# Rounds of scores between the projection slots of a gated recurrence, and a weight ring that runs on over the experts

## The reference

```python
def hgrn2_mixer(h, w_in, w_out, o_norm, lower_bound):
    q, f_logit, i_in, g = jnp.split((h @ w_in).astype(f32), 4, axis=-1)   # 4 x 1024 columns
    log_f = jnp.log(lb + (1.0 - lb) * jax.nn.sigmoid(f_logit))
    k = (1.0 - lb) * jax.nn.sigmoid(-f_logit)
    o = hgrn2_chunkwise(heads(q), heads(k), heads(i_in), heads(log_f))    # 8 heads of 128
    o = rms_norm(o, o_norm) * jax.nn.silu(heads(g))
    return o.reshape(B, S, ...).astype(h.dtype) @ w_out
...
        # b = running sum of log_f; scores[t,s] = sum_d q[t,d] k[s,d] exp(b[t,d] - b[s,d]), s <= t
        scores = jnp.einsum('bhtd,bhsd,bhtsd->bhts', qi, ki, jnp.exp(rel))
...
def moe_ffn(x, router, w_gu, w_down):
    for e in range(N_EXPERTS):                                            # 8 experts, 2 for each token
        y = y + combine[:, e:e + 1] * swiglu(xt, w_gu[e], w_down[e])
```

## Time and profile before

| | us |
|---|---|
| median of 3 runs | 2792.12 (2791.61 to 2793.78) |
| the profiled execution | 2794.28 |
| its span, first to last instruction | 2792.5 |
| TensorE busy | 2479.7 (89%) |
| VectorE busy | 1873.3 (67%) |
| ScalarE busy | 1322.0 (47%) |
| mean granted clock of TensorE | 0.943 |

### The profile page before, as it was taken

The page is one execution under the profiler, slowest core; times in us unless marked ns, Lnnn a source line. Parts: engine busy times, 40 slices in busy tenths (PEclk is TensorE's granted clock), DMA queues, the critical chain, the costliest instruction groups (busy, mean ns, idle before and its releaser), DMA issues.

```text
span 2792.5 us, 44521 instructions
## 1 busy us (share of the span) xinstructions
PE 2479.7 (89%) x17928; PEld 2334.3 (84%) x17928; DVE 1873.3 (67%) x2349; ACT 1322.0 (47%) x1408; POOL 308.8 (11%) x70
## 2 busy tenths in 40 slices
PE   6689789996678799789989788999999999999997
PEld 6579789996578699779978467989898999999996
DVE  5656575648556575742254657888888788888887
ACT  4434333334334233323322334766667676666674
POOL 0000063400000063345500000000000000000000
PEclk9899899998889899989999788999999999999999
DMA  5124135542034145445532014989888889889895
GB/s 204 61 91 150 69 144 182 189 140 103 0 119 146 61 167 182 151 144 179 186 120 77 1 61 157 361 327 343 320 331 337 335 325 335 335 325 342 327 341 206
DMA packets 77071, 556.56 MB, mean 199 GB/s; under 512 B 8544, under 2 KB 8672, under 8 KB 9952
## 3 DMA queue, kind: packets, MB, share of 16 engines
q1 hardware_dynamic: 75888, 547.45, 53.2%
q10 hardware_dynamic: 1008, 6.49, 0.6%
HBM read 552.86 MB, written 1.05 MB: 198 GB/s over the span
## 4 chain that ended last, share of the span: by engine, by line
PE 59%; DVE 5%; issue 2%; ACT 2%; DMA 0%; DVEq 0%; ACTq 0%
PE ps L1104 11%; PE ps L1106 11%; PE ps L1105 11%; PE ps L665 6%; PE ps L666 6%; PE ps L667 6%; PE ps L746 2%; PE ps L719 1%; PE ps L1144 1%; PE ps L1098 1%; DVE wlo L1229 1%; PE ps L800 1%; ACT whi L437 1%; PE ps L760 1%; PE ps L797 1%
## 5 line engine op out<-in xcount | busy, mean ns | idle before, releaser
L437 ACT ACTIVATE whi<-raw 128x2048 fp32r<-128x2048 f32 x519 | 992.0, 1914 | 737.8 <-PE ps L667 559.2
L1229 DVE TENSOR_TENSOR wlo<-raw,whi 128x2048 fp32r<-128x2048 f32 x453 | 1035.1, 2290 | 252.9 <-ACT whi L437 250.8
L665 PE MATMUL ps<-hh,whi 128*128 128x256 f32 x2336 | 679.7, 291 | 111.3 <-DVE hl L1297 94.8
L666 PE MATMUL ps<-hl,whi 128*128 128x256 f32 x2336 | 673.6, 288 | 0.0
L667 PE MATMUL ps<-hh,wlo 128*128 128x256 f32 x2336 | 672.9, 288 | 0.0
L665 PEld LDWEIGHTS ps<-hh,whi 128*128 128x128 f32 x2336 | 460.5, 197 | 117.8 <-issue 107.7
L1104 PE MATMUL ps<-whi,hh 128*128 128x256 f32 x1792 | 523.9, 292 | 15.3 <-issue 11.7
L1106 PE MATMUL ps<-wlo,hh 128*128 128x256 f32 x1792 | 507.7, 283 | 0.0
L1105 PE MATMUL ps<-whi,hl 128*128 128x256 f32 x1792 | 507.5, 283 | 0.0
L666 PEld LDWEIGHTS ps<-hl,whi 128*128 128x128 f32 x2336 | 460.9, 197 | 0.3
L667 PEld LDWEIGHTS ps<-hh,wlo 128*128 128x128 f32 x2336 | 460.4, 197 | 0.0
(11 more groups left out here) (313 smaller groups left out, 2737.0 us busy)
## 6 DMA issues: line engine op xcount, KB each, us to landing
raw<-stream SPq DMA_DIRECT2D x519, 1024.0 KB, 4.8
work<-w_in ACTq DMA_DIRECT2D x1, 2240.0 KB, 8.4
stage<-stage_consts ACTq DMA_DIRECT2D x4, 512.0 KB, 4.6
work<-mem_in ACTq DMA_DIRECT2D x2, 1024.0 KB, 5.5
x<-x_in SPq DMA_DIRECT2D x1, 1024.0 KB, 4.9
out<-x SPq DMA_DIRECT2D x4, 256.0 KB, 2.3
const<-consts SPq DMA_DIRECT2D x1, 548.5 KB, 5.8
par<-params SPq DMA_DIRECT2D x1, 405.5 KB, 6.4
```

The source lines that it names most:

```text
L437: nc.scalar.activation(whi[hi_at(g)][:, :], raw[g % RAWS][:, :], ACT.Copy).then_inc(hi_ready, 1)
L665: mm(out_ap, hi_w, hi_x, start=start, stop=False, **kw)
L666: mm(out_ap, hi_w, lo_x, start=False, stop=False, **kw)
L1229: V.tensor_tensor(wlo[g % RAWS][:, :], raw[g % RAWS][:, :], whi[hi_at(g)][:, :].bitcast(F32), ALU.subtract).then_inc(lo_ready[g % RAWS], 1)
```

## The change

**Recurrence.** The stream's order of `hg_in` changes: SyncE's loads are written out up to slot 180, and slots 0 to 3 fetch the weights of f, 4 to 7 those of q. The fills stand ahead of the phase. Sigmoids come in iteration 3, the logarithm (one operation a head, with factor and bias on ScalarE) and an Exp of it in iteration 4, keys in 4 (8 operations), the scan in 5. The nine rounds are made in the order `HG_ROUNDS`: diagonal, level 7, 0, 1 to 6. Round k's difference is made in iteration k+5 (rounds 2 and 3 in 6 and 7), its Exp in the same on ScalarE, its products in k+6, its matmuls after slot k+7, its masked copies in k+8. Differences are made with the right sign in two half-width operations (no Abs); level 7 needs no difference, since exp(b[t] - b[t-1]) is the forget factor itself. There are three difference buffers (`hg_d0`, `hg_d1` over the experts' activation buffers, and `hf`), one group of four banks, 4 to 7, for all rounds, and bank 3 for the values, which are turned in four parts after slots 9 to 12 and copied by ScalarE. Slots 8 to 15 are drained by ScalarE. The normalisation behind goes by quarters.

**Experts.** The ring doesn't start over; `few_expert` is written out on all engines (the other branch, which doesn't run, becomes a loop over pairs).

```diff
-        HG_D = [W(16, 8), hf[:, :]]
+        HG_D = [hg_d0[:, :], hg_d1[:, :], hf[:, :]]
+        HG_ROUNDS = ["diag", 7, 0, 1, 2, 3, 4, 5, 6]
...
-        def hi_at(g):
-
-            return (g if g < FIRST + PER_EXPERT else g - PER_EXPERT) % DEPTH
+        def hi_at(g, odd=0):
+
+            return (g + odd * PER_EXPERT) % DEPTH
...
-                    act.wait_ge(slot_used, e * PER_EXPERT + used_before(g))
-                nc.scalar.activation(whi[hi_at(g)][:, :], raw[g % RAWS][:, :], ACT.Copy).then_inc(hi_ready, 1)
+                    act.wait_ge(slot_used, e * PER_EXPERT + (g - DEPTH + 1))
+                nc.scalar.activation(whi[hi_at(g, odd)][:, :], raw[g % RAWS][:, :], ACT.Copy).then_inc(hi_ready, 1)
...
+            def after_hg_slot(s):
+                hg_scores(s - 7)
+                if 9 <= s <= 12:
+                    hg_turn_values(s - 9)
+
+            proj_pe("hg_in", 7, {s: lambda s=s: after_hg_slot(s) for s in range(7, hg.n)})
...
+                if 7 <= s <= 14:
+                    weigh(s - 6)
...
+                if s >= 8:
+                    keep(s - 8)
+                if s in (6, 7):
+                    decays(s - 4)
+                if 9 <= s <= 13:
+                    decays(s - 5)
+                split_lo(hg.g + s + AHEAD)
```

More of the change, by code:

```diff
@@ L365, in at_least, with source_of, expert_pairs @@
                 eng.wait_ge(s, value)
+        def source_of(g):
+            s = g - PHASES["hg_in"].g
+            return g + 4 if 0 <= s < 4 else (g - 4 if 4 <= s < 8 else g)
+        def expert_pairs(eng, body):
+            with eng.Fori(0, EXPERTS // 2) as pair:
+                for odd in range(2):
+                    body(pair * 2 + odd, odd)
         def wait_lo(eng, g, e=0):
@@ L578, in _ @@
+            for c in range(QUARTERS):
+                act.wait_ge(act_step, chain[0] - 3 + c)
+                nc.scalar.activation(W(8 + 2 * c, 2), W(8 + 2 * c, 2), ACT.Exp, scale=-0.5).then_inc(hg_orstd, 1)
             act.dma_start(stage[:, :], stage_consts[STAGE["pool"]]).then_inc(stage_loaded, 16)
@@ L625, in few_expert @@
                         bank, j = (gu.g + s) % BANKS, part * HALF + s
-                        if part == 0 and s == 2 and not first:
+                        if part == 0 and s == 2 and e:
                             few_keep_y(e - 1)
@@ L642, in _, with expert @@
                     nc.scalar.activation(Wc(FEW_GIVE + col, 512 * width), banks(bank, width), ACT.Copy).then_inc(spread_ready, 1)
-                few_expert(0, True)
-                with act.Fori(1, EXPERTS) as e:
-                    few_expert(e, False)
+                for e in range(EXPERTS):
+                    few_expert(e)
                 few_keep_y(EXPERTS - 1)
             with act.Else():
-                with act.Fori(0, EXPERTS) as e:
+                def expert(e, odd):
                     for part in range(2):
@@ L913, in _, with hg_turn_values @@
             norm_pe(4)
[L914 to L915 removed]
+            hg = PHASES["hg_in"]
+            def hg_turn_values(j):
+                pe.wait_ge(banks_drained, hg.e + 9 + j)
+                at_least(pe, hg_kept, j)
                 for tt in range(2):
[L917 to L920 removed]
@@ L923, in _ @@
-            proj_pe("hg_in", 7, {12: hg_turn_values})
-            pe.wait_ge(banks_drained, PHASES["hg_in"].e + PHASES["hg_in"].n)
-            def hg_scores(bank, lhs, rhs, tiles):
-                for h in range(8):
-                    for n, tt in enumerate(tiles):
-                        col = h * len(tiles) + n
-                        last = mm(ps[:, bank + col // 4, (col % 4) * P:(col % 4 + 1) * P], lhs(h, tt[0]), rhs(h, tt[1]), start=True, stop=True)
-                last.then_inc(hg_s, 1)
@@ L1128, in few_down @@
                 g = down.g + s
-                hi, lo = whi[hi_at(g)], wlo[g % RAWS]
+                hi, lo = whi[hi_at(g, e % 2)], wlo[g % RAWS]
                 wait_lo(pe, g, e)
@@ L1155, in few_expert @@
                             few_turn(gu, s - 1, e, part * HALF + s - 1)
-                    if part == 0 and not first:
+                    if part == 0 and e:
                         pe.wait_ge(y_kept, e)
@@ L1161, in few_expert @@
                             few_turn(gu, HALF - 1, e, part * HALF + HALF - 1)
-                        if part == 0 and not first and s in (1, 4):
+                        if part == 0 and e and s in (1, 4):
                             if s == 4:
@@ L1165, in few_expert @@
                             few_spread(e - 1, s // 4, 5)
-                        if part == 1 and s == 1 and not final:
-                            if not first:
+                        if part == 1 and s == 1 and e < EXPERTS - 1:
+                            if e:
                                 pe.wait_ge(y_added, e * 2 + 1)
@@ L1197, in _, with expert @@
                 acc_zero(True, False)
-                with pe.Fori(0, EXPERTS) as e:
+                def expert(e, odd):
                     for part in range(2):
@@ L1701, in _ @@
+            for c in range(QUARTERS):
+                gated(c)
+            sync()
+            staged(normed, to_hi(W(16, 8)), to_lo(W(16, 8)))
             xa(1, "hg_out")
```

353 lines of the change are left out of this document (199 added, 154 removed).

## The result

| | before | after |
|---|---|---|
| median | 2792.61 us (2791.61 to 2793.78, 4 runs) | 2710.49 us (2708.6 to 2710.99, 4 runs) |
| the profiled execution, its span | 2794.28, 2792.5 | 2710.58, 2708.8 |
| mean granted clock of TensorE | 0.943 | 0.948 |

After over before is 0.9705, 95% interval 0.9688 to 0.9721: 82 us less. The forecast was 2706; the time lies 4.5 us above it and inside the range. Between the spans of the two profiled executions the difference is 83.7 us (2792.5 - 2708.8); the sum had said 86.9.

A forecast was written before the change was run, and what follows sets the result against it. TensorE mostly waits for 106 us between the recurrence's projections and some 3 us per expert. Savings of 61.3 + 22.8 + 2.8 = 86.9 us give 2707.4 from the profiled execution, 2705.2 from the median; forecast 2706, range 2698 to 2722.

The forecast's parts named there:

- the sum: Whole kernel: savings in the recurrence, the experts and the last expert's end, 61.3 + 22.8 + 2.8 = 86.9 us.
- The gain in the recurrence: Rounds between projection slots, shorter normalisation: output projection starts at 717.0 instead of 778.33, 61.3 us.
- the first wait: Recurrence: TensorE waits 0.95 us for slot 7's drain, queued on VectorE behind scan, subtraction and remainders.
- The three turns: Recurrence: three turns of the values each wait 1.13 us for ScalarE's previous copy, queued behind Exp.
- no wait of TensorE over 2 us: Sign in the profile after, between slot 0 of the recurrence's input projection and the last round, ending near 699.5.
- the 24 matmuls with the values: Behind the last round: some 5.5 us, priced by the 3.82 us for 16 matmuls.
- The experts: Borders of experts: with the ring running on, 3.3 us less at each of seven borders, 22.8 us.
- late loads: Rival in the experts: weights come late at the borders, 22.8 us given back, 2729; chance 0.05 for experts not getting shorter.
- The end of the last expert: Copy of the last expert's result waits for only one unused slot's rounding and ends at 2763.8: 2.8 us saved.
- The rounds at the lower clock: Rival in the recurrence: rounds cost 5.46 us each and the time is 2716; chance 0.1.
- VectorE as the bound: Rival in slots with rounds: VectorE operations or waits cost 10% more, each slot grows 0.8 to 0.9 us, 2713; chance 0.1.
- Straight code as a loss: Rival in the experts: loading written-out code stalls ScalarE or VectorE, 94 us on top, 2800; chance 0.02.

The follow-up runs named there:

- log_first: The changed kernel with ScalarE's rounding of slot 8's weights moved behind the eight logarithms of iteration 4; 2707.51 us.
- rounds_behind: The changed kernel with its rounds of scores moved behind slot 15 of the projection on all three engines; 2759.47 us.
- dve_extra: The changed kernel with one more VectorE addition, about 1.2 us, in each of iterations 9 to 13 of the recurrence's projection; 2709.79 us.
- unroll_only: The kernel before with the experts written out on ScalarE and VectorE, the ring still starting over with each expert; 2796.93 us.
- after_again: The changed kernel run once more, unedited, as a base for later kernels; 2711.15 us.
- all_three: The changed kernel with value copies ahead of Exp, slot 8's rounding behind the logarithms, and the last expert's four unused slots not taken apart; 2698.58 us.

## Why the prediction was right, point by point

**The gain in the recurrence: right in place and mechanism, 3.5 us too large.** From slot 7's end to the end of the last round the sum had 85.0 us (614.5 to 699.5); the trace has 86.6 (613.22 to 699.85). The step that was off is the first wait, 2.50 and not 0.95. I had followed VectorE from the moment at which slot 0's drain lets it go, and had the scan start when that queue was free; in fact the scan starts at 604.43 with an idle time of 1.99 in front, waiting for the logarithms, which ScalarE takes behind the rounding of slot 8's weights. log_first moved just that and got 1.6 us back. The three turns wait 1.29 each and not 1.13, 0.5 more; TensorE's own work was 0.5 less than its 79.8. By this the prediction's own sign "no wait of TensorE over 2 us" up to the last round failed, at 2.50, without touching the mechanism. Its other signs held (last round's end at 699.85, rounds of 3.8 at 1.00, no Abs, experts of 129.3, no stop at a border), but `hg_out` came 58.9 us earlier and not 61.

From the last round's end to `hg_out` the sum had 17.5; it is 19.6. Nearly all of the difference is the 24 matmuls with the values: 7.2 us and not 5.5. They ran at a granted clock of 0.76. The windows of these matmuls and of the last spread in the changed kernel, and then of the same two in log_first (columns PE busy, granted clock, DMA, GB/s; the third window takes in seven records behind the 48):

```profile
702.40:709.50 7.10, 7.04 (x48) 0.76 0.00 0
...
2680.80:2687.20 6.40, 6.37 (x17) 0.57 0.03 6
```

```profile
701.40:708.40 7.00, 6.92 (x55) 1.00 0.00 0
...
2678.40:2682.20 3.80, 3.72 (x16) 1.00 0.03 6
```

I had priced them by rounds at full clock, and had kept the lower clock for the rounds alone. In the kernel before they took 5.6 us at 1.00, behind the same wait of 2.62, so its trace gave no sign of this term.

**The experts: right.** 22.8 us were forecast; the seven borders gave 23.3 (132.64 - 129.31 at each of six, and 3.4 at the last), 3.33 a border against 3.27, and expert 0, which has no border ahead of it, 0.3. VectorE was in time for the turn: none stands behind a wait. The end of the last expert gave 3.2 and not 2.8. What I had not said is how close the stream now is: I named late loads as an all-or-nothing rival at 2729, and in fact they take nothing in one execution and 2 to 6 us in another (above). By the windows the DMA engines' share rose from 0.89 to 0.91, as estimated.

**The end: missed.** From the last copy to the end nothing is changed, and the sum gave it nothing; the chances spoke of "some us either way through the clock". It took 2.2 us more, because the last spread ran at 0.57 (6.41 us; before 5.18 at 0.71) and the second sum of the final norm took 5.41 us (before 4.52): 1.2 and 0.9. In the executions profiled here the spread takes 3.72 (five kernels), 5.12, 5.18 (before), 5.41 (three), 6.37, 6.41 and 6.46 us, with the same code for it in all of them.

**The rivals.** The rounds at the lower clock didn't come: all nine ran at 1.00, though TensorE stood still for 2.50, 0.94 and three times 1.29 us among them. The Trainium skill's page "TensorE: Matmul & The Clock Gate", section "A second HAM failure mode: psum-queue depth-cycling", tells of a kernel that oscillates between the clocks through brief repeated idle times. Between slots this case's trace doesn't show it; behind the projection rounds_behind does, with idle times of 2.64 and 3.50 around rounds of 5.4 us and a mean clock of 0.73. VectorE as the bound fell with dve_extra. Straight code as a loss fell with unroll_only. The one load of a table on the path took 1.28 us, Exp starting 0.01 us behind it; the switch of 2.66 us, draining included, that the Trainium skill's page "ScalarE: Activation LUTs" gives in "What ACT_TABLE_LOAD costs" doesn't show here. ScalarE after:

```profile
711.63 2.42 ACT L630 ACTIVATE work<-ps,const 128x512 f32<-128x512 f32 x4
714.08 1.28 ACT L633 ACT_TABLE_LOAD   x1
715.37 0.63 ACT L633 ACTIVATE work<-work 128x512 f32<-128x512 f32 x1
```

What held the prediction together is that the terms that failed were small and the two large ones rest on the same kind of working: follow each engine's queue with measured durations, and ask at each step who is last. Some luck is in it too: against 3.5 lost in the recurrence and 2.2 at the end stand 1.3 more in the experts and 1.1 in the untouched start. The 0.8 us that I put on top of the sum (2706 instead of 2705.2) was far too little. The measured median is 5.3 above 2705.2: 3.2 by the sum's error, and 2.1 because the profiled execution before lay 2.2 above the median that I subtracted from, and the one after 0.1 above its own.

## What to carry to other kernels

Work whose steps wait for each other costs least between pieces of work that doesn't wait. Round 7 took 29 us here from its difference (663.96) to the end of its masked copies (693.1), about three times the 10.1 of a round before, and still cost only TensorE's 3.7, because what each engine does for one round fits into the time of a slot and a round. When a ring of buffers is written out for a loop, look at the seam: a ring whose length doesn't divide the loop's reuses a buffer too early once in each pass, and the wait shows up on an engine that has nothing to do with it. And once the order is right, look at what stands ahead of the last waited-for operation in its queue: two moves of a single operation, and leaving out four roundings and remainders that nobody uses, gave another 8 us here.

## What the runs showed that I had not expected

- The length of a wait doesn't decide the clock behind it. In two executions of the same kernel (the changed one and after_again) the last spread follows 3.33 and 3.38 us of idle time and ran at 0.57 (6.41 us) and 0.69 (5.41 us); in log_first it follows 3.30 and ran at 1.00 (3.72 us). The 24 matmuls with the values follow 2.6 us of idle time in all 13 traces. They ran at 1.00 in the three with the old recurrence, in log_first and in rounds_behind, at 0.79 in all_three, and at 0.76 in the other seven (1.6 us). There the two executions of the same kernel agree. What decides the clock was not found; a forecast of this kernel can't be better than these 2 to 4 us.
- Rounds of 128 x 128 float32 matmuls behind idle times of 0.9 to 2.5 us stayed at 1.00 as long as a projection slot stood between them, and fell to 0.73 on average without one. The idle times differ as well: in rounds_behind they are 2.64 us and more, and the one round there behind a shorter one, 1.21, took 3.81 us at 1.00. No run holds the one fixed and moves the other.
- With TensorE busy for 129.22 of 129.30 us and a stream of 341 GB/s beside it, single loads of 1 MB took 6.6 to 7.7 us on the chain in some executions and cost an expert up to 3.4 us, in four of ten traces. In the three traces whose experts took 132.6 to 132.8 us, none did.
- Writing out ScalarE's and VectorE's code for seven experts, the ring left as it was, cost 0.13 us an expert of 132.6.
